# The squares and roots of two RMS norms move from the head of their own stage to the tail of the stage in front

## The chip, the cores and the metric

One Trainium2 chip, one of its cores. The metric is the time of one execution on the device in microseconds (us). The kernel before was run three times: median 2228.65 us, lowest 2225.99, highest 2233.58.

## What is computed

A two-part transformer in fp32 over 256 tokens of width 1024. The change sits in the second part, which carries a latent stream x and a context stream ctx (256 tokens each) through two layers. Only this matters here:

```
def rmsnorm(x, w):
    xf = x.astype(jnp.float32)
    y = xf * lax.rsqrt(jnp.mean(xf * xf, axis=-1, keepdims=True) + EPS)
    return (y * w.astype(jnp.float32)).astype(x.dtype)
...
    for i in range(DEPTH_2):
        last = i == DEPTH_2 - 1
        ...
        h_lat = rmsnorm(x, norm1_w[i]) * (1.0 + sc1l) + sh1l
        h_ctx = rmsnorm(ctx, norm1_w[i]) * (1.0 + sc1c) + sh1c
        ...
        x = x + g1l * o_lat
        x = x + g2l * moe_ec(rmsnorm(x, norm2_w[i]) * (1.0 + sc2l) + sh2l,
                             moe_router_w[i], moe_w1[i], moe_w3[i], moe_w2[i])
        if not last:
            ctx = ctx + g1c * o_ctx
            ctx = ctx + g2c * moe_ec(rmsnorm(ctx, norm2_w[i]) * (1.0 + sc2c) + sh2c,
                                     moe_router_w[i], moe_w1[i], moe_w3[i], moe_w2[i])
    return rmsnorm(x, final_norm_w)
```

The first layer (i = 0) mixes with a state-space scan, the second (i = 1) with attention whose queries are latent tokens and whose keys are latent and context tokens. `moe_ec` has 16 experts of three 1024 x 1024 fp32 matrices, 12 MB an expert, and each expert picks 32 tokens. The norms of the change are the `norm1` of layer 1 (x and ctx, in front of attention) and the `norm2` of layer 1 (x alone, in front of the last expert layer).

## The kernel before

The program is a row of stages, each a `nc.Block()` with a list of instructions of its own for TensorE (PE), VectorE (DVE), ScalarE (ACT), GpSimd (POOL) and SyncE (SP). At the end of a block every engine meets the others at a barrier, and none starts the next block before all have arrived. Three stages matter: `expert_choice(0)` (called e0 here), the attention stage (L3182 to L3333) and `expert_choice(1)` (e1).

Activations lie in SBUF as tiles of 128 tokens x 1024 columns: `X[:, 0:2]` are the two tiles of x, `C[:, 0:2]` those of ctx, and `streams` lists C0, C1, X0, X1. Weights come through a ring of slots of 2 MB. SP issues their DMAs (`load_weights`, L356) in the order of use, and each waits in turn for the semaphore with which PE frees the slot. In e0 and e1 these are semaphores of the halves of the expert matrices (`half_used`, `h1_full`, `h3_full`, `y_full`).

A norm is an object of the class `NormT`. Its steps:

- `scalar_squares` (L432): ACT squares each tile of the stream with a running sum into one column of `eps_rows`, and writes the squares themselves into `xn`, where nobody reads them.
- `pool`, with the helper `root` (L364, L365): POOL turns each sum into 1/sqrt(sum + eps) in two instructions.
- `vector_scale` (L447): DVE scales each tile by its root into `xn`.
- `tensor` (L462): PE transposes the tiles into PSUM banks, eight blocks of 128 x 128 a tile, tile by tile.
- `evacuate` (L484 on DVE, L486 on ACT): the banks are copied, with the gain and bias of the modulation, into `hT`.

The attention stage has a norm of four tiles ("n5"), e1 one of two. In the lists of engines around them:

- The end of e0: the last expert's contribution is summed by PE (L2925) and added by DVE (L3145) in eight pieces of 128 x 512: C and X of token tile 0 (two each), then C and X of token tile 1. As soon as the first piece is added, PE runs four fp32 matmuls whose result nobody uses (`hold`, L511, recorded as eight instructions); these keep PE busy.
- The head of the attention stage: PE first makes the gate of the attention output by 16 small matmuls (`gate_banks`, L2044) into two banks, and then transposes, which needs all eight banks, these two included. ACT, behind its four squares, copies the two gate banks out (L598). Then come a `hold` of three and the projections (L585).
- The end of the attention stage: the output projection fills four banks (token tile 0, then 1; two halves each). DVE multiplies each by the gate (L3329) and adds it to X (L3331).
- The head of e1: PE runs a `hold` of four (L2831 and on), and only then the transposes:

```
                    if l == 1:
                        hold(pe, 4)
                    norm.tensor(pe)
```

  DVE clears and fills the router's operand (L3047, L3049) ahead of its scales. Then follow the router (L2842 to L3010), the choice of tokens on DVE (L3076 to L3099), the gathering of the chosen rows (L2880), and the experts (L2907).

Of the kernel before, what the change touches and what calls it, by code (L numbers as in the profile page):

```python
# [9 lines left out]
ACT = mybir.ActivationFunctionType  # L10
# [158 lines left out]
def build(nc, A, out):  # L169
# [15 lines left out]
    with ctx:  # L185
# [231 lines left out]
        class NormT:  # L417


            def __init__(self, tag, srcs, xn, hT, gain_col, bias_col=None, cols=None, apart=False, by=(DVE, ACTE)):  # L420
# [3 lines left out]
                self.T = len(srcs)  # L424

# [4 lines left out]
            def scalar_squares(self, act):  # L430
                for t, src in enumerate(self.srcs):
                    act.activation(self.xn[:, t, :], src, ACT.Square,  # L432
                                   accum_out=eps_rows[:, t:t + 1]).then_inc(squared, 1)

            def pool(self, pool):
                for t in range(self.T):
                    pool.wait_ge(squared, self.before + t + 1)
                    root(pool, t, 1, D, rooted)

            def vector_scale(self, dve):  # L440
                for t, src in enumerate(self.srcs):
                    dve.wait_ge(rooted, self.before + t + 1)
# [10 lines left out]
            def tensor(self, pe):  # L453
                m = self.per_bank()
                opened = [banks.open((self.tag, n), self.by[n % 2]) for n in range(KD // m)]
                for t in range(self.T):
                    pe.wait_ge(normed, self.before + t + 1)
                    for n, b in enumerate(opened):
                        if t == 0 and b.emptied:
                            pe.wait_ge(*b.emptied)  # L460
# [3 lines left out]
                        if t == self.T - 1:  # L464
                            i.then_inc(bank_full, 1)
# [2282 lines left out]
        early_at = []  # L2748

        def expert_choice(l):  # L2750
# [11 lines left out]
            with ExitStack() as scope:  # L2762
# [31 lines left out]
                norm = NormT(tag, [r for rs in res for r in rs], xn, hT, segs, apart=True)  # L2794
# [182 lines left out]
                def _(pool):  # L2977
                    norm.pool(pool)
# [24 lines left out]
                def _(act):  # L3003
                    norm.scalar_squares(act)
# [7 lines left out]
                    for e in range(N_EXP):  # L3012
# [24 lines left out]
                        act.activation(aT[:, :], psum[2][:, :], ACT.Copy).then_inc(aT_ready, 1)  # L3037
                    if l == 1:
# [128 lines left out]
                def _(sp):  # L3167
                    load_weights(sp)
                    if l == 1:
# [5 lines left out]
                        sp.wait_ge(out_stored, 16 * NT)  # L3175

        expert_choice(0)
# [4 lines left out]
        with ExitStack() as scope:  # L3182
# [22 lines left out]
            norm = NormT("n5", streams, shared, hT, mod_segments(1, 0))  # L3205
# [64 lines left out]
            def _(pool):  # L3270
                norm.pool(pool)
                qn.pool(pool)
                kn.pool(pool)

            @block.scalar
            def _(act):
                norm.scalar_squares(act)
# [14 lines left out]
                att.scalar(act)  # L3292

            @block.vector
            def _(dve):
# [28 lines left out]
                for t in range(NT):  # L3324
                    for n in range(2):
# [5 lines left out]
                        link(dve.tensor_tensor(X[:, t, c], X[:, t, c], part[:, n, :], ALU.add))  # L3331

# [4 lines left out]
        expert_choice(1)  # L3337
# [29 lines left out]
```

## Time and profile before

| | |
|---|---|
| median of three runs (lowest, highest) | 2228.65 us (2225.99, 2233.58) |
| profiled execution, span from first to last instruction | 2228.2 us (no time of its own beside it is shown) |
| instructions | 25120 |
| PE busy | 2031.3 us, 91% |
| DVE busy | 972.5 us, 44% |
| ACT busy | 648.4 us, 29% |
| POOL busy | 72.4 us, 3% |
| mean granted TensorE clock | 0.978 |
| HBM traffic | 623.57 MB by DMA, mean 280 GB/s |

How to read it: all times below are from the start of the span. e0 runs from 1095 to 1588 us, attention from 1588 to 1750, e1 from 1750 to the end. The share of busy time is a mean over stages with different limits, so each stage has to be read by itself. "Idle before" is time in which the engine waited, with what ended it. A releaser that ends in q (PEq, DVEq) is a sequencer's semaphore instruction, the barrier's among them. The granted clock is 1.00 or 0.50 (2.4 or 1.2 GHz); other values are means over a stretch that holds both.

### The profile page before, as it was taken

To read this page: it belongs to the slowest core of one execution; us is meant where nothing else is said; L and a number is where in the kernel's file an instruction comes from. 1 tells how busy PE (TensorE), PEld (TensorE's weight loads), DVE (VectorE), ACT (ScalarE), POOL (GpSimd) and SP (SyncE) were. 2 spreads that over 40 slices of the span, in tenths; PEclk is the share of its full clock that TensorE was granted. 3 is DMA by queue.
4 is the path that set the end of the run, shared out by engine and by line. 5 is a ranking of instruction groups with operands and counts; after the bars stand their busy time and mean duration, and the time that the engine had idled before them with its cause. 6 is when DMAs were issued, how large, how long until landed. Compare 5 with 4: busy or idle time off the path is not lost. (4 is left out here: it accounts for less than half of the span.)

```text
span 2228.2 us, 25120 instructions
## 1 busy us (share of the span) xinstructions
PE 2031.3 (91%) x10198; PEld 1076.7 (48%) x10198; DVE 972.5 (44%) x1668; ACT 648.4 (29%) x1284; POOL 72.4 (3%) x106
## 2 busy tenths in 40 slices
PE   6987987999899999999899999988899899999887
PEld 5844444444377888878643333322345422222222
DVE  4687224454688888882522221222466400001002
ACT  4243123111277667762211111100226111111100
POOL 0101010000000000000000000000120000000000
PEclk9998998999899999999999999999999999999999
DMA  8547567899433433322669999999830499999997
GB/s 291 204 147 264 189 248 291 341 397 382 125 97 95 131 115 114 110 99 76 281 265 428 427 428 427 427 427 429 332 147 1 175 428 426 427 425 427 426 426 300
DMA packets 147321, 623.57 MB, mean 280 GB/s; under 512 B 15460, under 2 KB 66151, under 8 KB 109063
## 3 DMA queue, kind: packets, MB, share of 16 engines
q1 hardware_dynamic: 142288, 601.65, 67.8%
q0 software_dynamic: 2352, 16.91, 2.0%
q10 hardware_dynamic: 2566, 3.41, 0.5%
q8 instruction: 81, 1.33, 0.2%
q14 instruction: 34, 0.27, 0.0%
HBM read 620.76 MB, written 1.18 MB: 279 GB/s over the span
## 5 line engine op out<-in xcount | busy, mean ns | idle before, releaser
L2907 PE MATMUL bank<-slots,xgTe 128*64 128x512 f32 (+1 forms) x1664 | 373.2, 595 | 31.9 <-DMA slots<-in_moe_w 31.8
L3128 DVE TENSOR_TENSOR actse<-sge,bank 32x512 f32<-32x512 f32 (+1 forms) x48 | 32.8, 682 | 498.0 <-PE bank L2907 278.8
L2907 PEld LDWEIGHTS bank<-slots,xgTe 128*64 128x64 f32 (+1 forms) x1664 | 107.5, 124 | 273.4 <-issue 229.0
L2907 PE MATMUL bank<-slots,aTe 128*64 128x512 f32 (+1 forms) x704 | 165.2, 612 | 13.9 <-issue 13.9
L3025 ACT ACTIVATE sge<-bank 32x512 f32<-32x512 f32 (+1 forms) x48 | 28.3, 590 | 480.3 <-PE bank L2907 480.1
L516 PE MATMUL bank<-slots_r 128*128 128x512 f32 x416 | 163.4, 393 | 0.0
L515 PE MATMUL bank<-hT_r,slots_r 128*128 128x512 f32 x384 | 155.6, 405 | 0.0
L517 PE MATMUL bank<-slots_r 128*128 128x512 f32 x384 | 152.0, 396 | 0.0
L585 PE MATMUL bank<-slots,hT 128*128 128x512 f32 (+1 forms) x320 | 133.2, 578 | 4.5 <-DVE hT L482 3.0
L2907 PEld LDWEIGHTS bank<-slots,aTe 128*64 128x64 f32 (+1 forms) x704 | 48.6, 129 | 113.9 <-issue 113.9
L3037 ACT ACTIVATE aTe<-bank 128x512 f32<-128x512 f32 x32 | 19.1, 597 | 275.2 <-PE bank L2964 275.2
L585 PEld LDWEIGHTS bank<-slots,hT 128*128 128x128 f32 x320 | 61.7, 194 | 74.4 <-issue 66.9
L2498 DVE SCALAR_TENSOR_TENSOR slots<-slots,vcols 128x512 f32<-128x512 f32 x128 | 95.5, 751 | 4.0 <-ACT slots L2350 0.3
L1692 PE MATMUL bank<-slots,hT 128*64 128x512 f32 x368 | 86.7, 605 | 9.9 <-ACT hT L1804 4.1
L2136 DVE TENSOR_TENSOR slots_r<-slots,slots_r 128x2048 fp32r<-128x2048 f32 x32 | 73.1, 2286 | 42.7 <-ACT slots_r L2131 42.6
L516 PEld LDWEIGHTS bank<-slots_r 128*128 128x128 f32 x416 | 78.3, 188 | 18.1
L517 PEld LDWEIGHTS bank<-slots_r 128*128 128x128 f32 x384 | 72.3, 188 | 17.6
L515 PEld LDWEIGHTS bank<-hT_r,slots_r 128*128 128x128 f32 x384 | 72.2, 188 | 16.7 <-issue 1.2
L515 PE MATMUL bank<-slots_r,hT_r 128*128 128x512 f32 (+1 forms) x192 | 74.9, 390 | 3.3 <-DVE hT_r L1070 3.3
L2367 ACT ACTIVATE rowsB<-rowsB,nb 128x128 f32<-128x128 f32 x256 | 76.5, 391 | 2.2 <-DVE rowsB L2624 2.2
L2131 ACT ACTIVATE slots_r<-slots 128x2048 fp32r<-128x2048 f32 x32 | 61.0, 1906 | 51.4 <-PE bank L517 51.4
L364 POOL TENSOR_SCALAR rstd<-eps_rows 128x1 f32<-128x1 f32 (+5 forms) x41 | 17.6, 430 | 1795.2 <-ACT xn L432 623.0
(571 smaller groups left out, 3159.0 us busy)
## 6 DMA issues: line engine op xcount, KB each, us to landing
slots<-in_moe_w SPq DMA_DIRECT2D x148, 2048.0 KB, 26.2
slots<-in_ada_w SPq DMA_DIRECT2D x24, 2048.0 KB, 12.1
extra0e<-in_moe_w SPq DMA_DIRECT2D x23, 2048.0 KB, 26.4
slots<-in_ssd_in_w SPq DMA_DIRECT2D x48, 512.0 KB, 5.3
slots<-in_moe_w_gate SPq DMA_DIRECT2D x23, 1024.0 KB, 10.4
slots<-in_moe_w_up SPq DMA_DIRECT2D x23, 1024.0 KB, 12.4
slots<-in_moe_w_down SPq DMA_DIRECT2D x23, 1024.0 KB, 7.4
rowsB<-acum_rows POOLq DMA_DIRECT2D x16, 1024.0 KB, 5.9
```

What stands on the lines that cost most here:

```text
L515: pe.matmul(out, lhsT[0], rhs[1], start=start, stop=False, skip_group_check=True)
L516: pe.matmul(out, lhsT[0], rhs[0], start=False, stop=False, skip_group_check=True)
L517: return pe.matmul(out, lhsT[1], rhs[0], start=False, stop=stop, skip_group_check=True)
L585: i = pe.matmul(b.ap[:, 0:width], lhsT(k), rhs(k), start=(k == 0), stop=(k == K - 1))
L1692: i = pe.matmul(b.ap[j * CAP1:(j + 1) * CAP1, :].rearrange("p (m n) -> p m n", m=2), xg[:, p // 2 % 2, k, at:at + CAP1], piece.ap.rearrang ...
L2131: act.activation(high_half(w), raw_half(w), ACT.Copy).then_inc(w_rounded, 1)
L2136: dve.tensor_tensor(low_half(w), raw_half(w), high_half(w).bitcast(F32), ALU.subtract).then_inc(w_split, 1)
L2367: i = act.activation(r, r, ACT.Exp, bias=nb[:, t, col:col + 1])
L2498: i = dve.scalar_tensor_tensor(o, padded[:, c, :, j:j + S], tap(j, CH(g)[c]), o, ALU.mult, ALU.add)
L2907: i = pe.matmul(bank[64 * n:64 * n + NJ * CAP, :], lhsT(4 * h + k), wv[:, 0, n * 512:(n + 1) * 512], start=(h == 0 and k == 0), stop=(h == ...
L3025: i = act.activation(sg[r_, :], psum[0][r_, :], ACT.Silu)
L3128: i = dve.tensor_tensor(acts[r_, :], sg[r_, :], psum[1][r_, :], ALU.mult)
```

## The change

Three things:

1. In e0, behind ACT's work for the last expert, ACT squares C0 and X0 as soon as DVE has added all pieces of token tile 0, and C1 and X1 after those of tile 1. POOL makes the four roots in e0 too. The attention stage starts with the scales; the order of the tiles there is C0, X0, C1, X1 (`order=[0, 2, 1, 3]`). The squares go to the `xn` of e0, which is free then.
2. In the attention stage, DVE counts up `residual_added` after each of the two token tiles, ACT squares X0 and X1 behind its last work of the stage and POOL makes their roots. The squares go to tiles of `xn5` that attention no longer uses.
3. `NormT` takes an order of its tiles, and its squares can be issued one at a time (`square`). e1 starts with the scales.

The number of squares, roots, scales and transposes stays the same.

```
--- before.py
+++ after.py
@@ -417,29 +417,33 @@
         class NormT:
 
 
-            def __init__(self, tag, srcs, xn, hT, gain_col, bias_col=None, cols=None, apart=False, by=(DVE, ACTE)):
+            def __init__(self, tag, srcs, xn, hT, gain_col, bias_col=None, cols=None, apart=False, by=(DVE, ACTE), order=None):
                 self.tag, self.srcs, self.xn, self.hT, self.by = tag, srcs, xn, hT, by
                 self.cols, self.apart = cols or (lambda k: slice(k * P, (k + 1) * P)), apart
                 self.gain_col, self.bias_col = gain_col, bias_col
                 self.T = len(srcs)
+                self.order = order or list(range(self.T))
 
                 self.before, self.nth = counted["streams"], counted["norms"] + 1
                 counted["streams"] += self.T
                 counted["norms"] += 1
 
             def scalar_squares(self, act):
-                for t, src in enumerate(self.srcs):
-                    act.activation(self.xn[:, t, :], src, ACT.Square,
-                                   accum_out=eps_rows[:, t:t + 1]).then_inc(squared, 1)
+                for t in self.order:
+                    self.square(act, t, self.xn[:, t, :])
+
+            def square(self, act, t, scratch):
+                act.activation(scratch, self.srcs[t], ACT.Square, accum_out=eps_rows[:, t:t + 1]).then_inc(squared, 1)
 
             def pool(self, pool):
-                for t in range(self.T):
-                    pool.wait_ge(squared, self.before + t + 1)
+                for n, t in enumerate(self.order):
+                    pool.wait_ge(squared, self.before + n + 1)
                     root(pool, t, 1, D, rooted)
 
             def vector_scale(self, dve):
-                for t, src in enumerate(self.srcs):
-                    dve.wait_ge(rooted, self.before + t + 1)
+                for n, t in enumerate(self.order):
+                    src = self.srcs[t]
+                    dve.wait_ge(rooted, self.before + n + 1)
                     dst = self.xn[:, t, :]
                     if self.apart:
                         dst = dst.rearrange("p (h j m) -> p h m j", h=2, j=4)
@@ -453,15 +457,15 @@
             def tensor(self, pe):
                 m = self.per_bank()
                 opened = [banks.open((self.tag, n), self.by[n % 2]) for n in range(KD // m)]
-                for t in range(self.T):
-                    pe.wait_ge(normed, self.before + t + 1)
+                for nth, t in enumerate(self.order):
+                    pe.wait_ge(normed, self.before + nth + 1)
                     for n, b in enumerate(opened):
-                        if t == 0 and b.emptied:
+                        if nth == 0 and b.emptied:
                             pe.wait_ge(*b.emptied)
                         for j in range(m):
                             i = pe.transpose(b.ap[:, (j * self.T + t) * P:(j * self.T + t + 1) * P],
                                              self.xn[:, t, self.cols(n * m + j)], ident)
-                        if t == self.T - 1:
+                        if nth == self.T - 1:
                             i.then_inc(bank_full, 1)
 
             def evacuate(self, eng, by):
@@ -2746,8 +2750,9 @@
         fin_loaded, f_squared, f_rooted, f_done, out_stored = (sem(x) for x in ("fin_loaded", "f_squared", "f_rooted", "f_done", "out_stored"))
 
         early_at = []
-
-        def expert_choice(l):
+        residual_added = sem("residual_added")
+
+        def expert_choice(l, norm=None):
 
             sid = (1, 0) if l == 0 else (0,)
             NJ = len(sid)
@@ -2791,7 +2796,11 @@
                     segs = mod_segments(0, 1)
                 else:
                     segs = lambda k: [(0, S, ncol[:, 1, 1, 0, k:k + 1], modcol[:, 1, 6 + k // 4, k % 4, 0:1])]
-                norm = NormT(tag, [r for rs in res for r in rs], xn, hT, segs, apart=True)
+                if l == 0:
+                    norm = NormT(tag, [r for rs in res for r in rs], xn, hT, segs, apart=True)
+                    following = NormT("n5", streams, None, hT, mod_segments(1, 0), order=[0, 2, 1, 3])
+                else:
+                    norm.xn, norm.gain_col = xn, segs
                 names = ("sub_ready_", "exp_ready_", "aff_ready_", "sv_ready_", "onehot_ready_", "gated_ready_", "fetched_",
                          "taken_", "gc_ready_", "half_used_", "h1_full_", "h3_full_", "silued_", "a_ready_", "gt_full_",
                          "tr_full_", "aT_ready_", "y_full_", "ye_ready_", "gs_ready_", "sc_full_", "sc_added_")
@@ -2975,7 +2984,9 @@
 
                 @block.gpsimd
                 def _(pool):
-                    norm.pool(pool)
+                    if l == 0:
+                        norm.pool(pool)
+                        following.pool(pool)
                     if l == 1:
                         for t in range(NT):
                             pool.wait_ge(f_squared, t + 1)
@@ -3001,7 +3012,8 @@
 
                 @block.scalar
                 def _(act):
-                    norm.scalar_squares(act)
+                    if l == 0:
+                        norm.scalar_squares(act)
                     norm.evacuate(act, ACTE)
                     act.wait_ge(sub_ready, 1)
                     act.activation(lg[:, :, :], lg[:, :, :], ACT.Exp).then_inc(exp_ready, 1)
@@ -3035,6 +3047,11 @@
                             i.then_inc(taken, 1)
                         act.wait_ge(tr_full, e + 1)
                         act.activation(aT[:, :], psum[2][:, :], ACT.Copy).then_inc(aT_ready, 1)
+                    if l == 0:
+                        for t in range(NT):
+                            act.wait_ge(sc_added, SC * (N_EXP - 1) + Q * (t + 1))
+                            for n in (t, NT + t):
+                                following.square(act, n, shared[:, n, :])
                     if l == 1:
                         for t in range(NT):
                             act.wait_ge(sc_added, Q * (t + 1))
@@ -3173,8 +3190,9 @@
                             sp.wait_ge(f_done, t + 1)
                             sp.dma_start(out["out"][0, t * P:(t + 1) * P, :], y[:, t, :]).then_inc(out_stored, 16)
                         sp.wait_ge(out_stored, 16 * NT)
-
-        expert_choice(0)
+                return following if l == 0 else None
+
+        norm_attn = expert_choice(0)
 
 
 
@@ -3202,7 +3220,9 @@
             sq = probs[:, :, :].rearrange("p a n -> p (a n)").rearrange("p (h d) -> p h d", d=64)
             tmp = pT5[:, 0:1024].rearrange("p (a h d) -> p a h d", a=2, h=16)
             oT = hflat[:, 0:2048].rearrange("p (k n) -> p k n", k=8)
-            norm = NormT("n5", streams, shared, hT, mod_segments(1, 0))
+            norm = norm_attn
+            norm.xn = shared
+            norm_e1 = NormT("e1", [X[:, t, :] for t in range(NT)], None, hT, None, apart=True)
             qh = q[:, :, :].rearrange("p t (h d) -> p t h d", d=64)
             kh = kk[:, :, :].rearrange("p t (h d) -> p t h d", d=64)
             QU = [(n, t) for n in range(2) for t in range(NT)]
@@ -3268,13 +3288,12 @@
 
             @block.gpsimd
             def _(pool):
-                norm.pool(pool)
                 qn.pool(pool)
                 kn.pool(pool)
+                norm_e1.pool(pool)
 
             @block.scalar
             def _(act):
-                norm.scalar_squares(act)
                 for n in range(2):
                     copy_out(act, ACTE, ("g15", 0, n), g1[:, n * 512:(n + 1) * 512], 512)
                 norm.evacuate(act, ACTE)
@@ -3290,6 +3309,9 @@
                 for g in range(1, KVH, 2):
                     copy_out(act, ACTE, ("kT5", g), kT[:, g, :], 512)
                 att.scalar(act)
+                for t in range(NT):
+                    act.wait_ge(residual_added, t + 1)
+                    norm_e1.square(act, t, shared[:, 2 + t, :])
 
             @block.vector
             def _(dve):
@@ -3329,12 +3351,13 @@
                         dve.tensor_tensor(part[:, n, :], b.ap[:, :], g1[:, c], ALU.mult).then_inc(emptied[DVE], 1)
                         dve.wait_ge(emptied[DVE], b.done)
                         link(dve.tensor_tensor(X[:, t, c], X[:, t, c], part[:, n, :], ALU.add))
+                    dve.sem_inc(residual_added, 1)
 
             @block.sync
             def _(sp):
                 load_weights(sp)
 
-        expert_choice(1)
+        expert_choice(1, norm_e1)
```

Where ACT's instructions stand at the end of e0 and the head of the attention stage. `L2762` is the end of e0's list before (`L2767` after), `waits ..._release` the barrier. Before:

```order
L3037 ACTIVATE aTe<-bank 128x512 [waits tr_full_e0]
L2762 UNCONDITIONAL_BRANCH
L3275 UNCONDITIONAL_BRANCH [waits barrier_Pool_Activation_PE_DVE_SP_release]
L432 ACTIVATE xn,eps_rows<-C 128x1024 x2
L432 ACTIVATE xn,eps_rows<-X 128x1024 x2
L598 ACTIVATE g<-bank 128x512 [waits bank_full] x2
L486 ACTIVATE hT<-bank,modcol,ncol 128x256 [waits bank_full]
```

and in the change, where line numbers are up to 20 higher:

```order
L3049 ACTIVATE aTe<-bank 128x512 [waits tr_full_e0]
L436 ACTIVATE xne,eps_rows<-C 128x1024 [waits sc_added_e0]
L436 ACTIVATE xne,eps_rows<-X 128x1024
L436 ACTIVATE xne,eps_rows<-C 128x1024 [waits sc_added_e0]
L436 ACTIVATE xne,eps_rows<-X 128x1024
L2767 UNCONDITIONAL_BRANCH
L3295 UNCONDITIONAL_BRANCH [waits barrier_Pool_Activation_PE_DVE_SP_release]
L602 ACTIVATE g<-bank 128x512 [waits bank_full] x2
L490 ACTIVATE hT<-bank,modcol,ncol 128x256 [waits bank_full]
```

The four squares stand ahead of the barrier, each pair behind a wait for DVE's additions, and the copies of the gate banks are now ACT's first work of the attention stage.

POOL at the end of the attention stage and the head of e1, as one piece of the difference (the rows without a sign, with `squared`, are the two roots of e1's norm, the f_squared row belongs to the norm at the end of the program):

```order
 L364 TENSOR_SCALAR rstd<-eps_rows 128x4 [waits heads_summed]
 L365 TENSOR_TENSOR rstd<-rstd,minus_half 128x4 [waits pool_step]
-L3182 UNCONDITIONAL_BRANCH
-L2976 UNCONDITIONAL_BRANCH [waits barrier_Pool_Activation_PE_DVE_SP_gather]
 L364 TENSOR_SCALAR rstd<-eps_rows 128x1 [waits squared]
 L365 TENSOR_TENSOR rstd<-rstd,minus_half 128x1 [waits pool_step]
 L364 TENSOR_SCALAR rstd<-eps_rows 128x1 [waits squared]
 L365 TENSOR_TENSOR rstd<-rstd,minus_half 128x1 [waits pool_step]
+L3200 UNCONDITIONAL_BRANCH
+L2985 UNCONDITIONAL_BRANCH [waits barrier_Pool_Activation_PE_DVE_SP_gather]
 L364 TENSOR_SCALAR rstd<-eps_rows 128x1 [waits f_squared]
```

The barrier moved from ahead of the two roots to behind them. PE's list is the same row for row in both programs.

## Rows read from the trace of the kernel before

**Rows 1.** Busy time by stage, e1: PE, PEld, DVE, ACT, POOL, clock, DMA share, GB/s

```profile
1750.00:2228.00 478.00, 429.66 (x1980) 136.94 (x1980) 66.48 (x117) 59.18 (x139) 5.05 (x8) 0.97 0.95 403
```

**Rows 2.** Chain that ended last, near the end: start, us, what

```profile
2153.76 37.06 DMA slots<-in_moe_w
```

**Rows 3.** Busy time in two stretches of e1's head, columns as in Rows 1

```profile
1770.00:1775.00 5.00, 4.74 (x38) 3.99 (x40) 3.14 (x10) 0.86 (x3) 0.00 (x0) 1.00 0.02 7
1775.00:1780.00 5.00, 5.00 (x26) 1.32 (x24) 0.83 (x2) 2.32 (x5) 0.00 (x0) 1.00 0.32 69
```

**Rows 4.** Timeline of SP: start, us, engine, line, transfer, count

```profile
1585.06 2.67 SPq L356 DMA_DIRECT2D slots<-in_moe_w  x1
...
1748.20 0.80 SPq L356 DMA_DIRECT2D slots<-in_moe_w  x2
...
1777.70 3.76 SPq L356 DMA_DIRECT2D slots<-in_moe_w  x2
```

**Rows 5.** Timeline of DVE, ACT and POOL, end of e0 and head of attention

```profile
1586.06 0.68 DVE L3145 TENSOR_TENSOR X<-X,bank 128x512 f32<-128x512 f32 x1
...
1588.15 1.06 ACT L432 ACTIVATE xn<-C 128x1024 f32<-128x1024 f32 x1 [16.73 <-PEq L2762]
...
1589.69 0.57 POOL L365 TENSOR_TENSOR rstd<-rstd,minus_half 128x1 f32<-128x1 f32 x1
...
1591.28 1.04 ACT L432 ACTIVATE xn<-X 128x1024 f32<-128x1024 f32 x1
...
1592.32 1.05 ACT L598 ACTIVATE g<-bank 128x512 f32<-128x512 f32 x2
...
1594.24 0.75 DVE L447 TENSOR_SCALAR xn<-X,rstd 128x1024 f32<-128x1024 f32 x1 [0.46 <-POOL rstd L365]
```

**Rows 6.** Timeline of PE, same place

```profile
1582.61 3.70 PE L511 MATMUL bank<-consts 128*128 128x512 f32 x8
1588.17 2.02 PE L2044 MATMUL bank<-consts,modcol 128*128 128x128 f32 x16 [1.86 <-PEq L2762]
...
1593.43 2.95 PE L462 MATMUL bank<-consts,xn 128*128 128x128 f32 x25 [0.15 <-ACT g L598]
...
1599.87 55.17 PE L585 MATMUL bank<-slots,hT 128*128 128x512 f32 x128 [0.33 <-ACT hT L486]
```

**Rows 7.** Timeline of DVE, ACT and POOL, end of attention and head of e1

```profile
1735.27 0.69 DVE L3331 TENSOR_TENSOR X<-X,part 128x512 f32<-128x512 f32 x1
...
1749.00 0.69 DVE L3331 TENSOR_TENSOR X<-X,part 128x512 f32<-128x512 f32 x1
...
1750.22 1.06 ACT L432 ACTIVATE xne<-X 128x1024 f32<-128x1024 f32 x1 [32.39 <-PEq L3182]
...
1751.77 0.58 POOL L365 TENSOR_TENSOR rstd<-rstd,minus_half 128x1 f32<-128x1 f32 x1
...
1752.38 1.31 DVE L447 TENSOR_SCALAR xne<-X,rstd 128x1024 f32<-128x1024 f32 x1 [1.52 <-POOL rstd L365]
```

**Rows 8.** Timeline of PE, same place

```profile
1750.24 3.67 PE L511 MATMUL bank<-consts 128*128 128x512 f32 x8 [2.07 <-PEq L3182]
...
1755.76 1.09 PE L462 MATMUL bank<-consts,xne 128*128 128x128 f32 x8 [0.92 <-DVE xne L447]
```

**Rows 9.** PE in stretches: length, busy (count), granted clock, DMA share, GB/s

```profile
472.70:476.00 3.30, 3.30 (x10) 0.50 1.02 422
476.00:479.40 3.40, 3.40 (x18) 0.99 1.02 431
...
1595.60:1599.00 3.40, 3.08 (x14) 1.00 1.05 420
...
1750.20:1753.90 3.70, 3.66 (x9) 1.00 0.96 399
```

**Rows 10.** Timeline of PE, two places with a pause ahead of them

```profile
471.78 6.64 PE L1692 MATMUL bank<-slots,hT 128*64 128x512 f32 x22 [2.33 <-issue]
...
1098.44 6.62 PE L462 MATMUL bank<-consts,xne 128*128 128x128 f32 x32 [5.28 <-DVE xne L447]
```

More of the change, by code:

```diff
@@ L424, in __init__ @@
                 self.T = len(srcs)
+                self.order = order or list(range(self.T))
                 self.before, self.nth = counted["streams"], counted["norms"] + 1
@@ L430, in scalar_squares, with square @@
             def scalar_squares(self, act):
[L431 to L433 removed]
+                for t in self.order:
+                    self.square(act, t, self.xn[:, t, :])
+            def square(self, act, t, scratch):
+                act.activation(scratch, self.srcs[t], ACT.Square, accum_out=eps_rows[:, t:t + 1]).then_inc(squared, 1)
             def pool(self, pool):
[L436 to L437 removed]
+                for n, t in enumerate(self.order):
+                    pool.wait_ge(squared, self.before + n + 1)
                     root(pool, t, 1, D, rooted)
             def vector_scale(self, dve):
[L441 to L442 removed]
+                for n, t in enumerate(self.order):
+                    src = self.srcs[t]
+                    dve.wait_ge(rooted, self.before + n + 1)
                     dst = self.xn[:, t, :]
@@ L455, in tensor @@
                 opened = [banks.open((self.tag, n), self.by[n % 2]) for n in range(KD // m)]
-                for t in range(self.T):
-                    pe.wait_ge(normed, self.before + t + 1)
+                for nth, t in enumerate(self.order):
+                    pe.wait_ge(normed, self.before + nth + 1)
                     for n, b in enumerate(opened):
-                        if t == 0 and b.emptied:
+                        if nth == 0 and b.emptied:
                             pe.wait_ge(*b.emptied)
@@ L3037, in _ @@
                         act.activation(aT[:, :], psum[2][:, :], ACT.Copy).then_inc(aT_ready, 1)
+                    if l == 0:
+                        for t in range(NT):
+                            act.wait_ge(sc_added, SC * (N_EXP - 1) + Q * (t + 1))
+                            for n in (t, NT + t):
+                                following.square(act, n, shared[:, n, :])
                     if l == 1:
@@ L3204, in build @@
             oT = hflat[:, 0:2048].rearrange("p (k n) -> p k n", k=8)
-            norm = NormT("n5", streams, shared, hT, mod_segments(1, 0))
+            norm = norm_attn
+            norm.xn = shared
+            norm_e1 = NormT("e1", [X[:, t, :] for t in range(NT)], None, hT, None, apart=True)
             qh = q[:, :, :].rearrange("p t (h d) -> p t h d", d=64)
@@ L3292, in _ @@
                 att.scalar(act)
+                for t in range(NT):
+                    act.wait_ge(residual_added, t + 1)
+                    norm_e1.square(act, t, shared[:, 2 + t, :])
             @block.vector
```

29 lines of the change are left out of this document (19 added, 10 removed).

## Prediction

> **What bounds the kernel.** I read the stages first, then the end of the chain, then the two boundaries that the change touches. In the busy times of the last stage the DMA engines are in use 95% of the time at 403 GB/s, with PE busy for 429.66 of 478 us [rows 1]. Near its end the chain of waits runs through a transfer of 37.06 us [rows 2]. So the weights' stream sets the end of e1, and an engine that gets faster inside the expert loop gains nothing. But the stream has a hole: between 1770 and 1775 us it moves 7 GB/s and between 1775 and 1780 only 69 [rows 3], since all slots are full and the first is freed by the first expert's half; SP issues the next transfer at 1777.70 [rows 4]. Whatever moves that first half moves the rest of the stream with it, one to one. The attention stage has no such cover and no such limit: from 1599.87 PE works for 55.17 us in one piece after a wait for ACT's evacuation [rows 6], so its end too moves with its head. Both boundaries therefore count in full, and the question is what ends last at each.
>
> **What ends last at each boundary, before.** End of e0: DVE's last addition ends at 1586.74 [rows 5], but SP is in an issue until 1587.73 [rows 4], and the next stage starts at 1588.15 [rows 5], 0.4 us after SP. In the attention stage the squares look like the head of the path: the four take 4.2 us, 1588.15 to 1592.32, and the last scale ends at 1594.99 [rows 5]. But PE's transposes wait for something else: the 25 of the long piece start at 1593.43, released by ACT's copy of the gate bank, and end at 1596.38 [rows 6]. The copies start at 1592.32 only because they stand behind the squares [rows 5]. PE's own work there is 2.02 us of gate matmuls [rows 6] and 32 transposes at 2.95/25 = 0.118 us, 3.8 us: 5.8 us in all. End of attention: DVE ends at 1749.69, the next stage starts at 1750.22, 0.5 us later [rows 7]. PE runs its hold for 3.67 us to 1753.91, during which squares, roots and first scale (1752.38 to 1753.69 [rows 7]) are made; the second tile's transposes start at 1755.76, released by DVE [rows 8].
>
> **The change at the end of e0.** It moves four squares, four roots and the barrier. The squares of tile 0 lie beside DVE's additions of tile 1 and cost nothing; were those additions gone, they would cost the 2.1 us that two squares take. Those of tile 1 start behind the last addition, at 1586.80. A square's start to its root's end is 1588.15 to 1590.26, 2.1 us [rows 5]; the second starts one square (1.04) later, so the last root ends at 1586.80 + 1.04 + 2.1 = 1589.95. SP has long arrived by then, so its 1.0 us of lateness goes unused. With 0.5 us for the barrier (the gap at the other boundary; 0.4 behind SP here; I take 0.5 since it is the longer) the attention stage starts at 1590.45 instead of 1588.15: 2.3 us later. DVE scales four tiles back to back, 4 x 0.75 = 3.0 us, done at 1593.45 instead of 1594.99. That is the gain meant, 1.5 us, and PE hides it: gate matmuls to 1592.47; six transposes; the copy of the second gate bank, half of 1.05 us, ends about 1593.1; so the long run of transposes starts at 1593.2 instead of 1593.43. Term: **-0.2 us**. Evacuation, hold and projections follow from there.
>
> **The change at the end of attention.** X0 is final at 1735.96 [rows 7], its square and root are free; on ACT and POOL nothing is queued behind the wait. The added semaphore counts on DVE lie in its wait for PE. The square of X1 starts at about 1749.8, its root ends 2.1 us later at 1751.9 (the same interval here: 1750.22 to 1752.35 [rows 7]), the barrier opens at 1752.4, 2.2 us later than before. DVE is served: two small fills, then two scales of 1.31 us [rows 7], done at 1755.5 instead of about 1755.7. PE is not: its hold of 3.67 us [rows 8], which before lay beside the squares and the roots, now starts at 1752.4 and ends at 1756.1, and nothing is left for it to lie beside but the scales. Then come all sixteen transposes; the second tile's start at 1757.05 (1.0 us for the first eight) instead of 1755.76. Term: **+1.3 us**. SP's transfer that stands behind this barrier is issued 2.2 us later, which costs nothing, as two of 2 MB were issued at 1748.20 [rows 4] and take 10 us at 403 GB/s. If those were not there, the 2.2 us would be added to the stream.
>
> **The clock.** The pauses of PE at the barriers grow: before, 1.86 us [rows 6] and 2.07 us [rows 8], and the clock stays at 1.00 behind them (1750.20 to 1753.90 [rows 9]). After, PE ends its hold at 1586.3 and starts at 1590.45, and ends the projection at 1748.2 and starts at 1752.4: 4.2 us each. Behind a pause of 2.33 us [rows 10] the granted clock is 0.50 (1.2 GHz) from 472.70 to 476.00, with 10 matmuls instead of the 18 of the next stretch [rows 9]. Behind one of 5.28 us, 32 transposes take 6.62 us [rows 10] instead of 3.8. So pauses of 4.2 us, between these two, will very likely bring one stretch at half clock each. A stretch of 3.3 us that loses 8 of 18 matmuls costs 1.5 us if it lies wholly on PE's work, and nothing if it ends in the pause. I take 1.2 us each, nearer the upper end, as PE's work starts late in the pause's wake: **+2.4 us**; ends 0 and 3.0.
>
> The Trainium skill (TensorE: Matmul & The Clock Gate, Part 4: PE-mode transpose) says that transposes do not count as busy work for the clock gate. By that rule the clock would stay low through the 32 transposes, which is the slower rival below. The trace speaks against it: right behind 25 of them the clock is still 1.00 (1595.60 to 1599.00 [rows 9]).
>
> Sum: -0.2 + 1.3 + 2.4 = +3.5 us on the span of 2228.2, so 2231.7. The median of the runs is 0.45 us above that span, so **2232.1 us**, 0.16% more. The scatter of the three runs is larger than that; 0.3% (6.7 us) is about the least that a measurement of this kernel can tell from no change.
>
> **Rivals.**
> - *The clock holds.* For it: it held at 2.07 us. Against it: it fell at 2.33. Then -0.2 + 1.3: 2229.8 us. Chance 0.12.
> - *The gain arrives*: the scales, not PE's fixed work, set the pace, as when gate matmuls and hold are overtaken or the barrier opens sooner than 0.5 us behind POOL. Then 1.5 us less at the first and 0.2 at the second boundary: 2227.0. Against it: PE's list is the same row for row. Chance 0.08.
> - *Slower: the clock stays low from the barrier until the transposes are over.* Gate matmuls +2.0, transposes 6.62 - 3.8 = +2.8, hold +3.7, sixteen transposes +1.4, with -0.2 and +1.3: +11.0, so 2239.7, slower by 0.5%. It decides once the half clock lasts through about 13 us of PE's work in both places together. For it: rows 10, where 5.28 us of pause doubled most of 6.62 us. Against it: the pause here is shorter, and what follows is not transposes first but matmuls. Chance 0.10.
> - *The stages are not moved by their heads* (another wait takes up the shift, so that the time is 2228.7). Against it: the hole in rows 3. Chance 0.05.
>
> The forecast itself, one short stretch at half clock or nearly so at each boundary, has 0.60, and what is left, 0.05, is scatter. The first rivals and the forecast lie from 2227.0 to 2233.7; with 1.5 us of scatter of a median below and part of the slow rival above, the range is 2225.5 to 2238. No mechanism gives a gain of 0.3%; only scatter does: 0.05. Slower by over 0.3%: the slow rival and scatter on top of the forecast, 0.14. Within: 0.81.
>
> **What would show it.** In the profile after: four squares ahead of the barrier with DVE's additions beside two of them; POOL's last root about 3.2 us behind the last addition, and the next stage's first instruction 0.5 us later; PE's gate matmuls followed by transposes with at most one short wait for ACT; DVE done with its scales while PE still runs its hold at the head of e1; pauses of PE of about 4 us at both barriers, and a granted clock of 0.50 just behind them; the hole in the stream longer by 1 to 4 us. It is wrong if the attention stage's projections start more than 1 us earlier against DVE's last addition than before (13.1 us, 1586.74 to 1599.87), if the first expert does not shift, or if a wait for weights appears in the attention stage.

## The result, and the profile after

The changed kernel is slightly slower: median 2235.07 us (2232.53 to 2243.56, 16 runs) against 2228.4 (2225.49 to 2233.97, 16 runs) for the kernel before, ratio 1.0034, 95% interval 1.0026 to 1.0042. That is +7.6 us, 5.8 to 9.4. The forecast was 2232.1: the time is within its range but 3 us above it, and the forecast change of +3.5 us is about half of the measured one. The ratio of 0.34% lies on the bound of 0.3% that I had given 0.81 to stay within; its interval holds that bound, so the runs don't say on which side of it the change is.

The profiled execution has a span of 2232.9 us, 4.7 more than before. Spans differ by some 2 us before the change is even reached, so I compare four intervals instead. They run from mark to mark: **first**, DVE's last addition of e0 (its end) to the first projection; **second**, the attention's last addition (its end) to DVE's first evacuation in e1; **gather**, from there to the first expert's matmul; **experts**, from there to the end.

| kernel (one profile each) | first | second | gather | experts |
|---|---|---|---|---|
| before | 13.13 | 6.54 | 17.79 | 454.14 |
| after | 15.03 | 10.11 | 19.42 | 454.18 |
| difference | +1.90 | +3.57 | +1.63 | +0.04 |

The first three differences come to +7.1 us, inside the measured 5.8 to 9.4. The attention stage between the marks is the same within 0.4 us (149.83 and 149.43), and no wait for weights appears in it. The whole difference from the first mark to the end is therefore +6.7 us. These are two profiles only; the table of the experiments shows how far such sums can be from the times.

DVE, ACT and POOL at the first boundary, after (timeline: start, us, engine, line, operation):

```profile
1584.02 0.68 DVE L3162 TENSOR_TENSOR X<-X,bank 128x512 f32<-128x512 f32 x1
...
1588.23 0.75 DVE L451 TENSOR_SCALAR xn<-C,rstd 128x1024 f32<-128x1024 f32 x1 [3.53 <-PEq L2767]
1588.90 0.75 DVE L451 TENSOR_SCALAR xn<-X,rstd 128x1024 f32<-128x1024 f32 x1
1589.56 0.75 DVE L451 TENSOR_SCALAR xn<-C,rstd 128x1024 f32<-128x1024 f32 x1
1590.23 0.75 DVE L451 TENSOR_SCALAR xn<-X,rstd 128x1024 f32<-128x1024 f32 x1
1595.51 3.71 DVE L488 TENSOR_SCALAR hT<-bank,ncol,modcol 128x256 f32<-128x256 f32 x8 [4.54 <-PE bank L466]
...
1584.73 1.06 ACT L436 ACTIVATE xne<-C 128x1024 f32<-128x1024 f32 x1 [0.20 <-DVE X L3162]
...
1585.79 1.04 ACT L436 ACTIVATE xne<-X 128x1024 f32<-128x1024 f32 x1
...
1587.31 0.57 POOL L365 TENSOR_TENSOR rstd<-rstd,minus_half 128x1 f32<-128x1 f32 x1
```

The change does what it says. The last addition ends at 1584.70, the last root at 1587.88, 3.2 us later as reckoned, the barrier opens 0.35 us behind it, and DVE makes its four scales back to back and is done at 1590.98, 6.3 us behind the last addition where it was 8.25 before [rows 5]. Then it waits 4.54 us for PE. The gain meant is there, and it is lost to PE, whose timeline is:

```profile
1580.57 3.70 PE L515 MATMUL bank<-consts 128*128 128x512 f32 x8
1588.23 3.75 PE L2048 MATMUL bank<-consts,modcol 128*128 128x128 f32 x16 [3.96 <-PEq L2767]
1591.77 4.46 PE L466 MATMUL bank<-consts,xn 128*128 128x128 f32 x32
...
1599.73 4.53 PE L589 MATMUL bank<-slots,hT 128*128 128x512 f32 x10 [0.33 <-ACT hT L490]
```

The pause ahead of the gate matmuls is 3.96 us (1.86 before [rows 6]), and they take 3.75 us instead of 2.02. The same at the second boundary, PE and DVE:

```profile
1751.72 6.41 PE L515 MATMUL bank<-consts 128*128 128x512 f32 x8 [4.10 <-PEq L3200]
1757.97 1.91 PE L466 MATMUL bank<-consts,xne 128*128 128x128 f32 x16
...
1752.26 2.23 DVE L451 TENSOR_SCALAR xne<-X,rstd 128x1024 f32<-128x1024 f32 x2
1759.27 1.90 DVE L488 TENSOR_SCALAR hT<-bank,ncol,modcol 128x256 f32<-128x256 f32 x4 [4.79 <-PE bank L466]
```

DVE is done with both scales at 1754.49; PE is in its hold until 1758. The hold takes 6.41 us instead of 3.67 [rows 8]. The clock in stretches (columns: length, busy and count of PE, PEld, DVE, ACT, POOL, clock, DMA share, GB/s):

```profile
1586.60:1593.40 6.80, 5.17 (x24) 5.20 (x25) 2.74 (x4) 1.51 (x4) 1.03 (x3) 0.50 1.03 400
1750.50:1757.20 6.70, 5.48 (x7) 2.41 (x8) 2.64 (x4) 0.00 (x0) 0.79 (x2) 0.50 1.01 429
1774.30:1777.70 3.40, 3.40 (x19) 3.40 (x18) 1.49 (x5) 0.00 (x0) 0.00 (x0) 0.50 0.00 0
...
1775.00:1780.00 5.00, 5.00 (x29) 3.94 (x29) 3.33 (x8) 1.20 (x4) 0.00 (x0) 0.73 0.00 0
1780.00:1785.00 5.00, 5.00 (x26) 1.40 (x24) 0.00 (x0) 1.98 (x4) 0.00 (x0) 1.00 0.37 88
```

Half clock (1.2 GHz) for 6.8 us at each barrier, beginning 1.3 and 1.7 us before PE starts again, and for 3.4 us on the gathering. There the 32 matmuls take 5.47 us instead of 3.84, which is the whole of the third difference. The hole in the stream [rows 3] is now longer: it reaches to SP's issue at 1782.36, where it was 1777.70 [rows 4]. No packet of weights moves for 13.3 us (1770.02 to 1783.36), where it was 8.0 (1770.68 to 1778.69), and from there the stream needs what it needed before.

### The profile page after: what moved, and what is told of

Read it like the earlier page. It is cut to its first block and busy times, and to the rows that moved or that the text cites. A ratio compares the mean times of both kernels' runs of the same rounds, so it can differ in the third digit from the quotient of the medians.

```text
span 2232.9 us, 25120 instructions
## 1 busy us (share of the span) xinstructions
PE 2034.8 (91%) x10198; PEld 1078.3 (48%) x10198; DVE 972.0 (44%) x1668; ACT 649.5 (29%) x1284; POOL 70.4 (3%) x106
```

## The experiments

The table holds all results. Ratios are to executions of the kernel before that were timed beside each kernel, with 95% intervals; each kernel was executed 11 to 16 times, the last two once. "By intervals" is the sum of the first three against before (37.46 us), as a share of 2228, from one profile each. "Clock" is the mean granted clock over a whole execution, as a mean of all executions; the kernel before had 0.9787 or 0.9788 beside e1 to e8.

| kernel | first | second | gather | experts | by intervals | clock | ratio (interval) |
|---|---|---|---|---|---|---|---|
| after | 15.03 | 10.11 | 19.42 | 454.18 | +0.32% | 0.9754 | 1.0034 (1.0026 to 1.0042) |
| e1_first_only | 14.19 | 7.04 | 19.42 | 454.18 | +0.14% | 0.9761 | 1.0023 (1.0012 to 1.0033) |
| e2_second_only | 13.19 | 9.07 | 19.42 | 457.40 | +0.19% | 0.9771 | 1.0027 (1.0016 to 1.0037) |
| e3_no_head_hold | 15.04 | 6.78 | 19.62 | 454.56 | +0.18% | 0.9749 | 1.0022 (1.0011 to 1.0032) |
| e4_filled | 12.69 | 7.37 | 17.80 | 457.45 | +0.02% | 0.9786 | 1.0001 (0.9991 to 1.0011) |
| e5_hold_moved | 12.68 | 5.93 | 19.42 | 456.33 | +0.03% | 0.9776 | 1.0011 (1.0002 to 1.0020) |
| e6_gates_moved | 12.14 | 6.78 | 19.63 | 457.15 | +0.05% | 0.9777 | 1.0006 (0.9996 to 1.0016) |
| e7_copies_on_vector | 12.82 | 6.46 | 17.79 | 454.38 | -0.02% | 0.9775 | 1.0014 (1.0005 to 1.0023) |
| e8_no_pause | 11.64 | 5.98 | 17.80 | 456.66 | -0.09% | 0.9780 | 1.0002 (0.9993 to 1.0011) |
| r_after (one execution) | 15.11 | 10.14 | 19.42 | 454.40 | +0.32% | 0.975 | 2236.42 us |
| r_before (one execution) | 13.17 | 6.48 | 17.79 | 457.93 | 0.00% | 0.978 | 2233.34 us |

In eight of the nine kernels the ratio lies above the sum of intervals, by up to 0.16% or 3.5 us (e7_copies_on_vector). Where that time goes isn't shown: one profile stands for all executions of a kernel, and the four intervals leave out what lies ahead of the first mark. So the intervals show what an edit does at a boundary, and only the ratio shows the whole time.

**e1_first_only** and **e2_second_only** each undo one half of the change, by giving that norm back its squares and roots at the head of its own stage. The first piece is from e1_first_only, the second from e2_second_only; the lines that issue squares and roots move back with them:

```
-                    norm.xn, norm.gain_col = xn, segs
+                    norm = NormT(tag, [r for rs in res for r in rs], xn, hT, segs, apart=True)
...
-            norm = norm_attn
-            norm.xn = shared
+            norm = NormT("n5", streams, shared, hT, mod_segments(1, 0))
```

> Only the four squares and roots of the attention stage's norm are moved; the norm of the last expert layer is as before. Own theory (PE's fixed work behind the barrier, at half clock): from DVE's last addition of the first expert layer to the first projection 15.0 us as in the changed kernel (13.1 before); from the attention's last addition to the first evacuation 6.5 us as before; whole time +2 us against before, ratio 1.001. Rival (the later opening of the barrier itself costs, the same at both places): about half of the 6.7 us, ratio 1.0015. Rival (only the second boundary costs): no difference from before.

> Only the two squares and roots of the last expert layer's norm are moved; attention's norm is as before. Own theory: 13.1 us from last addition to projection, 10.1 us from the attention's last addition to the first evacuation (6.5 before), of which 1.3 us is the hold that has lost its cover and the rest clock; whole time +3.6 us and up to 1.6 more where a further stretch at half clock falls on the gathering of rows, ratio 1.002. Rival (barrier alone): as the other half, 1.0015.

Both halves cost, as the timings say by themselves; the rival by which only the second costs has fallen. The size of each depends on the execution's clock. In e1_first_only the half clock behind the first barrier lasted from 1587.97 for 3.4 us, and the first interval is 14.19, not 15.0; in e2_second_only it lasted 3.4 us too, and the second is 9.07. And in e1_first_only the second boundary, which is that of the kernel before with a pause of 2.07 us, met half clock as well. The halves come to 0.50% together where the whole change has 0.34%, so their sizes don't add up in the times; by intervals they do (0.33% and 0.32%). The PE of e1_first_only:

```profile
1586.52 2.43 PE L2048 MATMUL bank<-consts,modcol 128*128 128x128 f32 x16 [3.96 <-PEq L2766]
1588.74 4.96 PE L466 MATMUL bank<-consts,xn 128*128 128x128 f32 x32
...
1747.14 5.37 PE L515 MATMUL bank<-consts 128*128 128x512 f32 x8 [2.07 <-PEq L3198]
```

The 1.7 us that this hold took longer moved the interval by 0.5 us only, since the second tile's transposes wait for DVE's scale there in any case. The rival "the barrier costs the same at both" isn't excluded by the two ratios, which overlap; e4_filled decides that.

**e3_no_head_hold**: PE's unused work at the head of e1 taken out of the changed kernel.

```
-                    if l == 1:
-                        hold(pe, 4)
                     norm.tensor(pe)
```

> The changed kernel without the four matmuls of hold at the head of the last expert stage (they compute nothing that is used). If this work of PE is what ends last there, the interval from the attention's last addition to the first evacuation falls from 10.1 us to about 6.0 (barrier 2.6, two fills 0.6, two scales 2.2, the second tile's first transposes 0.5), and the time by 4 us, less 1 to 3 us for a clock that stays at half for longer, since PE does less behind the pause. If DVE's scales or the barrier end last, the interval stays near 10 and the time is that of the changed kernel.

```profile
1753.77 3.67 PE L466 MATMUL bank<-consts,xne 128*128 128x128 f32 x16 [5.87 <-DVE xne L451]
```

```profile
1750.80:1757.50 6.70, 3.73 (x18) 0.50 1.00 427
```

The second interval falls from 10.11 to 6.78 us: the hold was what ended last. The expected 6.0 is missed by 0.8, since the half clock now falls on the transposes. (The first fence is PE's timeline; the second a stretch: length, PE's busy time and count, clock, DMA share, GB/s.) PE now pauses for 5.87 us, and the transposes run wholly at half clock, 3.67 us instead of 1.91. As a repair it is worth little: ratio 1.0022.

**e4_filled**: PE kept at work up to both barriers, with matmuls that compute nothing that is used. Below it PE's timeline.

```
-                        hold(pe, 4, psum[4])
+                        hold(pe, 8, psum[4])
...
                 w0.freed = w1.freed = (bank_full, b.full)
+                hold(pe, 4)
```

> The changed kernel with PE kept at work up to both barriers: eight matmuls of hold instead of four at the end of the first expert layer, four more at the end of attention; the hold at the head of the last stage stays. If the pause brings the half clock, the granted clock behind both barriers is now 1.00, the first interval falls from 15.0 to 12.9 us and the second from 10.1 to 7.9, and the time by 4 to 6 us, to before +1 (ratio 1.0005). If the clock is low for another reason, or the barrier itself is the cost, both intervals stay within 0.5 us of the changed kernel.

```profile
1581.51 7.13 PE L515 MATMUL bank<-consts 128*128 128x512 f32 x16
1589.17 2.02 PE L2048 MATMUL bank<-consts,modcol 128*128 128x128 f32 x16 [0.53 <-PEq L2767]
1591.03 3.81 PE L466 MATMUL bank<-consts,xn 128*128 128x128 f32 x32
...
1750.76 3.67 PE L515 MATMUL bank<-consts 128*128 128x512 f32 x8 [0.66 <-PEq L3200]
1754.27 1.91 PE L466 MATMUL bank<-consts,xne 128*128 128x128 f32 x16
```

This settles that the long pause is what brings the clock down here. The barrier opens as late as in the changed kernel (3.53 us behind the last addition), and nothing but PE's unused work is altered, but the pauses are 0.53 and 0.66 us, everything behind them runs at the full rate (2.02, 3.67 and 1.91 us), and the cost is gone within what the runs resolve: ratio 1.0001, at most 0.11%. Nor is it one profile alone: over all executions the granted clock is 0.9786, that of before, against 0.9754 in the changed kernel. So the clock is 15.03 - 12.69 = 2.3 us at the first boundary and 10.11 - 7.37 = 2.7 at the second. What is left of the change without it is -0.44 and +0.83 us. The rival "the barrier's later opening is itself the cost" has fallen.

**e5_hold_moved**: e4 without the hold at e1's head, so that it has moved to the end of attention.

> The filled kernel (holds up to both barriers) without the hold at the head of the last stage. First interval as in the filled kernel, 12.7 us. At the second the barrier opens 2.6 us behind the last addition, then fills 0.6, two scales 2.3, 0.5 until the first bank is full: 6.0 to 6.2 us to the first evacuation, at full clock, against 7.4 filled, 10.1 changed and 6.5 before. Time 0.9 us below before by the two intervals, ratio 0.9996, which is no measurable difference. If the barrier's later opening is a cost of its own, the second interval stays above 6.5 us.

```profile
1752.17 2.21 PE L466 MATMUL bank<-consts,xne 128*128 128x128 f32 x16 [2.43 <-DVE xne L451]
```

The second interval is 5.93 us, below the 6.54 of before: here the gain meant for the second norm arrives, in an execution in which the clock stayed at 1.00 behind a pause of 2.43 us (PE's timeline above). The gathering met a half clock stretch in this profile (19.42). The time doesn't show the gain; its ratio of 1.0011 is 2.4 us above before where the intervals give 0.6.

**e6_gates_moved**: e5's second boundary, and the gate matmuls moved from the head of attention to the tail of e0.

```
                         hold(pe, 4, psum[4])
+                        pe.wait_ge(sc_added, SC * N_EXP)
+                        gate_banks(pe, "g15", 1, 2, 0, ACTE)
+                        hold(pe, 2, psum[4])
...
-                gate_banks(pe, "g15", 1, 2, 0, ACTE)
                 norm.tensor(pe)
```

> The kernel with the hold moved, and the 16 gate matmuls also taken out of the head of the attention stage into the tail of the first expert layer, behind the last addition, followed by a hold of two in place of four. PE's work behind the barrier is then the 32 transposes alone. If PE's fixed work is what hid the gain, the first interval falls to 10.8 to 11.3 us (barrier 3.5, first scale 0.75, transposes 3.8 and then 3.2 as in the filled kernel), 2 us below before, and the time to 2.5 us below before, ratio 0.999. If DVE's scales or ACT's copies end last instead, it stays at 12.7.

```profile
1584.74 2.05 PE L2048 MATMUL bank<-consts,modcol 128*128 128x128 f32 x16 [0.48 <-DVE X L3163]
1586.62 1.88 PE L515 MATMUL bank<-consts 128*128 128x512 f32 x4
1589.61 3.71 PE L466 MATMUL bank<-consts,xn 128*128 128x128 f32 x32 [1.11 <-DVE xn L451]
```

The direction is right and the size a miss: 12.14 us, not 10.8 to 11.3. The hold of two ends at 1588.50, later than POOL's last root, so PE itself arrives last and the barrier opens 4.1 us behind the last addition (1584.68). PE's work no longer bounds the transposes; DVE's first scale does.

Its second boundary is the code of e5_hold_moved, and yet the interval is 6.78 us instead of 5.93. PE there, and two stretches with the columns of those above:

```profile
1750.66 3.44 PE L466 MATMUL bank<-consts,xne 128*128 128x128 f32 x16 [2.44 <-DVE xne L451]
```

```profile
1750.70:1753.70 3.00, 3.00 (x15) 3.00 (x15) 1.59 (x3) 0.18 (x1) 0.00 (x0) 0.50 1.03 434
1753.80:1757.10 3.30, 2.65 (x23) 1.12 (x21) 2.06 (x5) 1.65 (x4) 0.00 (x0) 1.00 1.01 432
```

The same pause, 2.44 us, was followed by half clock here. Without a hold at its head, the gain at this boundary comes and goes with the clock.

**e7_copies_on_vector**: the kernel before, with the gate banks copied by DVE ahead of its scales rather than by ACT behind its squares.

```
-                gate_banks(pe, "g15", 1, 2, 0, ACTE)
+                gate_banks(pe, "g15", 1, 2, 0, DVE)
```

> The kernel before with the two copies of the gate banks on VectorE, ahead of its scales, in place of ScalarE behind its squares. If the transposes waited for these copies and not for the squares, as I read it, the transposes now follow each scale, the last scale ends about 0.3 us later than before or at the same time, and the first interval becomes 12.8 to 13.2 us, so that the squares' chain is next in line right behind the copies. If the copies were no bound, nothing changes but the order: 13.1 us. Time as before within 0.5 us in both cases; the releaser named at the transposes tells them apart (scale or copy).

```profile
1590.91 4.34 PE L462 MATMUL bank<-consts,xn 128*128 128x128 f32 x32 [1.45 <-DVE xn L447]
```

The wait for the copies ([rows 6]: 25 transposes released by ACT) is gone, the transposes follow DVE's scales, and the interval is 12.82 us: the copies were the bound, with the squares' chain 0.3 us behind them. The ratio of 1.0014 doesn't fit an interval sum below before; what these 3 us are is open. The granted clock of its executions, 0.9775 against 0.9788, points to more half clock in them, but no profile shows where.

**e8_no_pause**: e6 with `hold(pe, 1, psum[4])` in place of two behind the gate matmuls, and `hold(pe, 2)` at e1's head in place of none.

> Both boundaries mended after what the last two runs showed. First: gate matmuls in the tail of the first expert layer, and one matmul of hold behind them in place of two, so that PE no longer arrives last at the barrier: it opens 3.5 us behind the last addition instead of 4.1, the first interval is 11.5 to 11.7 us (13.1 before). Second: hold of four in the tail of attention, and a hold of two at the head of the last stage, which lies beside the fills and the first scale: 5.9 to 6.0 us (6.5 before), with the clock at 1.00 and no more than 17.9 us from the first evacuation to the first expert. Together 2.1 us below before if the expert stage takes its 454.2 us, ratio 0.999; up to 3 us more where stretches at half clock fall on its start and its end. Rival (the barrier is the cost): no gain, ratio 1.001 or more.

```profile
1580.54 2.05 PE L2048 MATMUL bank<-consts,modcol 128*128 128x128 f32 x16 [0.48 <-DVE X L3165]
1582.43 1.02 PE L515 MATMUL bank<-consts 128*128 128x512 f32 x2
1584.83 3.71 PE L466 MATMUL bank<-consts,xn 128*128 128x128 f32 x32 [1.38 <-DVE xn L451]
...
1744.13 1.96 PE L515 MATMUL bank<-consts 128*128 128x512 f32 x4 [0.66 <-PEq L3203]
1745.97 2.19 PE L466 MATMUL bank<-consts,xne 128*128 128x128 f32 x16
```

Each interval came out as reckoned: 11.64, 5.98 and 17.80 us, 2.0 us less than before in all, at full clock behind both barriers. The timing cannot tell it from the kernel before (1.0002, 0.9993 to 1.0011). So the moved norms can be made to pay at both boundaries, but by about 0.1%, which is below what these runs resolve. No version here is shown to beat the kernel before. And the gate matmuls were never moved with the norms left in place, so how much of the 11.64 us is owed to the moved norms isn't shown either.

**r_after** and **r_before**: both kernels once more, one execution each.

> The changed kernel once more, unchanged, for a second profile: the two intervals again 14.2 to 15.1 and 9.1 to 10.2 us with half clock behind both barriers, if the pause sets the clock and not chance. The stretch from the first evacuation to the first expert (19.4 against 17.8 us) and the expert stage (454.2 or 457.4) may come out either way, since I hold them for chance.

> The kernel before once more, unchanged: intervals 13.1 and 6.5 us with the clock at 1.00 behind both barriers. The stretch from the first evacuation to the first expert and the expert stage may come out either way; 19.4 here would show that the 1.6 us are chance and no part of the change.

r_after repeats the first three intervals within 0.1 us. r_before shows two things. Its experts take 457.93 us, with nothing changed, so a difference of 3 us in that interval needs no edit; whether an edit makes it more frequent isn't shown. And the half clock came behind its first barrier too, after a pause of 1.89 us; PE there, and then the stretch, with the columns of the one above:

```profile
1587.78 3.47 PE L2044 MATMUL bank<-consts,modcol 128*128 128x128 f32 x16 [1.89 <-PEq L2762]
...
1593.04 2.95 PE L462 MATMUL bank<-consts,xn 128*128 128x128 f32 x25 [0.16 <-ACT g L598]
```

```profile
1588.20:1591.40 3.20, 3.20 (x17) 0.50 1.04 406
```

Yet its first interval is 13.17 us. In the kernel before, the gate matmuls end 2.1 us before ACT starts its copies (1590.19 and 1592.32, [rows 5, 6]), and what a slow stretch adds falls into this slack. The change takes the slack away: the barrier opens 2.1 us later against the last addition (3.53 us, 1.41 before), the copies no longer stand behind squares, and PE's work is left bare.

## Why the prediction was right and where it fell short

- **That both stages move with their heads** held: both halves of the change show in the times, and the hole in the stream became longer, by 5.3 us where I had 1 to 4.
- **When the barrier opens** held at both: 3.53 us behind the last addition (reckoned 3.7) and 2.57 (2.7).
- **PE's fixed work hides the gain** held. DVE finished 4.5 and 4.8 us ahead of its next work, waiting for PE. Without the clock the two terms are -0.44 and +0.83 (e4_filled), +0.4 together, where I had -0.2 and +1.3, +1.1 together.
- **The clock term was mis-sized, and this is the step that failed.** I had "+2.4 us; ends 0 and 3.0", 1.2 for each boundary, from one stretch of 3.3 us at half clock. Measured: 2.3 and 2.7, 5.1 together. The half clock lasted 6.8 us in both profiles of the changed kernel, not 3.3. My own rows 10 pointed there: the pause of 5.28 us had been followed by half clock through most of 6.62 us of transposes. I used that row for the slower rival only, although the expected pause of 4.2 us lay between the two rows; its upper end belonged into the term's bounds.
- **A place was missing from the sum**: the gathering, +1.63 us, which is the clock's too. A half clock stretch fell on its 32 matmuls in both profiles of the changed kernel and in neither of before. It came in every profile with half clock behind the second barrier, and in one (e5_hold_moved) without. Why the two go together wasn't tried.
- **The slower rival** (the clock stays low through all the transposes, +11.0 us) was right in kind and too large. In the after profile the clock is 1.00 from 1593.5 on, with PE in the middle of its transposes.
- **Two figures of the prediction don't come out of its own terms.** The forecast's upper end is -0.2 + 1.3 + 3.0 = +4.1 us, so 2232.8, where it says 2233.7. And the work that the slower rival names (gate matmuls, hold and all transposes) is about 11 us at full clock, not 13. Neither changes the forecast.
- **That the clock holds at 2.07 us and falls at 2.33** was no safe reading of two pauses. It fell after 1.89 us in r_before and after 2.07 in e1_first_only, and it held after 2.43 in e5_hold_moved. At a boundary as it was before the change, the two falls cost 0.0 and 0.5 us.

The chances: 0.81 for within 0.3% was too sure. With the terms as measured (-0.44 + 0.83 + 5.1 + 1.6) the sum is +7.1 us, at the edge of that bound. The time lies within the range, but not because the sum was right: the range was wide for the scatter and for part of the slower rival, and the clock's missing 4.3 us fell into that room.

## What to carry to other kernels

When work is moved ahead of a barrier to shorten the head of a stage, list for each engine what it still has to do behind the barrier: the head gets shorter only if the longest of these lists does, and here PE's gate matmuls, hold and transposes were the longest, covered until then by the very squares that were moved. A barrier that opens later also lengthens PE's pause, and the half clock that came with it here fell on exposed work; keep PE busy up to the barrier, or put its independent work (here the gate matmuls) into the wait, but stop early enough that PE doesn't arrive last (e6 against e8). A filler placed behind a barrier is free only while something slower runs beside it.

## What the runs showed of the hardware

- All seven pauses of 4.0 to 4.1 us at the two boundaries went with half clock, for 3.4 us in some profiles (e1, e2) and 6.8 in others (after, r_after, e3). The long ones began 1.2 to 1.7 us before PE started again, the short ones 0.1 and 1.5 us after. Of eight pauses of 1.9 to 2.1 us two did (r_before first, e1 second), and of two of 2.4 us in the same code one (e6, not e5). A term for the clock is a spread, not a number.
- The Trainium skill (TensorE: Matmul & The Clock Gate, Part 4: PE-mode transpose) says that transposes don't count as busy for the clock gate in the way that other work does, and that full clock doesn't engage for them. The traces here do not agree for these fp32 transposes. In the changed kernel's stretch below PE does nothing else, and the clock, at 0.50 just before, is full. There the gate matmuls had run ahead of them. In e6_gates_moved's stretches above nothing else had: behind the pause of 2.44 us PE runs transposes alone, from 1750.66, at half clock, and the clock is back at 1.00 by 1753.8, before the sixteen are over.

```profile
1593.50:1596.20 2.70, 2.70 (x25) 2.50 (x23) 0.69 (x2) 0.58 (x2) 0.00 (x0) 1.00 1.03 413
```

- In the expert stage, where the weights' stream sets the end, a half clock stretch at one place goes with a longer time. All six profiles with a stretch that begins 18.4 to 19.3 us behind the first expert's start (r_before, e2, e4, e5, e6, e8) have 456.3 to 457.9 us; the other six, without it, have 454.1 to 454.6, though all of them have such stretches elsewhere in the stage. That is a pattern in twelve profiles; that the stretch is the cause was not tested by an edit.
